# Low parts, one-hot matrices by token pairs, 16-bit index selection and 12 tiles per top-k round in a mixer and expert kernel

## The reference

```
q = (h @ w_query) as [token, 8 heads, 2, 128]
s = q . subkeys                        # 128 scores for each head and half
sv, si = top_k(s, 16)                  # per half
cand   = sv[0][:, None] + sv[1][None]  # 256 sums per head
top_s, pos = top_k(cand, 16)
experts = si[0][pos // 16] * 128 + si[1][pos % 16]
gates   = softmax(top_s)
hid = gelu(u_table[experts] . h) * gates
y   = sum over the 128 chosen of hid * v_table[experts]
```

## Time and profile before

| | |
|---|---|
| median of 3 runs | 3415.35 us (3414.62 to 3419.66) |
| the profiled execution | 3417.07 us, its span 3415.3 us |
| busy share of the span | TensorE 92%, VectorE 70%, GpSimd 38%, ScalarE 34% |
| granted TensorE clock, mean | 0.961 |
| DMA | 542.36 MB, mean 159 GB/s |

### The profile page before, as it was taken

One profiled execution on the slowest core, in us unless ns is written; L12 is line 12 of the kernel. 1 busy time (PEld: TensorE's weight loads), 2 busy tenths in 40 slices (PEclk: granted clock), 3 DMA queues, 4 the chain that ended last, 5 costly groups with the idle time before them and its releaser, 6 DMA issues.

```text
span 3415.3 us, 44166 instructions
## 1 busy us (share of the span) xinstructions
PE 3138.1 (92%) x16765; PEld 2770.9 (81%) x16765; DVE 2400.1 (70%) x3304; ACT 1171.7 (34%) x1668; POOL 1294.8 (38%) x607
## 2 busy tenths in 40 slices
PE   8999997687778777999999999999999999999999
PEld 8788896677777766999999888888888777788887
DVE  6676299999999948799999757454444534445573
ACT  4452343233333332333333332233332435423322
POOL 2303365466676657788888200010000431132000
PEclk9999998898888888999999999999999999999999
DMA  5111354367777688999998133233332321123332
GB/s 171 59 44 56 96 185 134 106 185 248 246 243 232 221 269 303 348 343 343 344 334 314 56 95 96 92 99 95 96 98 91 97 86 38 44 69 95 95 93 93
DMA packets 188077, 542.36 MB, mean 159 GB/s; under 512 B 17696, under 2 KB 77472, under 8 KB 187296
## 3 DMA queue, kind: packets, MB, share of 16 engines
q1 hardware_dynamic: 150112, 403.59, 36.4%
q0 software_dynamic: 36864, 134.23, 11.3%
q10 hardware_dynamic: 960, 2.65, 0.3%
...
...
## 4 chain that ended last, share of the span: by engine, by line
PE 57%; DVE 29%; issue 6%; DMA 5%; ACT 2%; POOL 1%; SPq 0%; DVEq 0%; ACTq 0%
PE ring_banks L295 16%; PE ring_banks L297 16%; PE ring_banks L296 16%; DVE oneI L2874 4%; DVE ge L2896 3%; DVE u_row L2847 3%; DVE row_sum L2857 3%; DMA u_row<-u_rows,row_numbers 2%; DVE glo L2902 2%; DVE vlo L2909 2%; DMA slot<-u 2%; DVE oneJ L2870 1%; DVE hits L2871 1%; PE ring_banks L1635 1%; PE work_banks L1604 1%
## 5 line engine op out<-in xcount | busy, mean ns | idle before, releaser
L915 POOL TENSOR_TENSOR wlo<-slot,whi 128x1024 fp32r<-128x1024 f32 x247 | 650.0, 2636 | 1578.4 <-ACT whi L1747 1577.2
L295 PE MATMUL ring_banks<-xx,wlo 128*128 128x512 f32 (+2 forms) x2704 | 1016.7, 376 | 21.3 <-POOL wlo L915 19.4
L297 PE MATMUL ring_banks<-xx,whi 128*128 128x512 f32 (+2 forms) x2704 | 1002.8, 371 | 0.0
L296 PE MATMUL ring_banks<-xx,whi 128*128 128x512 f32 (+2 forms) x2256 | 832.5, 369 | 0.0
L1747 ACT ACTIVATE whi<-slot 128x1024 fp32r<-128x1024 f32 x427 | 451.5, 1059 | 979.9 <-DMA slot<-w 574.9
L295 PEld LDWEIGHTS ring_banks<-xx,wlo 128*128 128x128 f32 x2704 | 521.8, 193 | 86.5 <-POOL wlo L915 19.8
L297 PEld LDWEIGHTS ring_banks<-xx,whi 128*128 128x128 f32 x2704 | 519.1, 192 | 63.3
L296 PEld LDWEIGHTS ring_banks<-xx,whi 128*128 128x128 f32 x2256 | 436.1, 193 | 46.9 <-issue 0.2
L2322 DVE TENSOR_TENSOR wlo<-slot,whi 128x1024 fp32r<-128x1024 f32 x180 | 220.3, 1224 | 137.2 <-ACT whi L1747 127.3
L2847 DVE SCALAR_TENSOR_TENSOR u_row<-u_row,token_rows 128x1024 f32<-128x1024 f32 x128 | 215.0, 1706 | 75.2 <-DMA u_row<-u_rows,row_numbers 75.1
L2117 ACT ACTIVATE vhi<-v 128x1024 fp32r<-128x1024 f32 x128 | 135.2, 1061 | 335.7 <-DMA v<-v 335.5
...
## 6 DMA issues: line engine op xcount, KB each, us to landing
slot<-w SPq DMA_DIRECT2D x301, 512.0 KB, 3.6
slot<-u SPq DMA_DIRECT2D x128, 512.0 KB, 4.1
v<-v SPq DMA_DIRECT2D x128, 512.0 KB, 7.0
early<-early SPq DMA_DIRECT2D x128, 192.0 KB, 3.9
...
gates<-stage SPq DMA_DIRECT2D x47, 512.0 KB, 5.2
...
```

The source lines that it names most:

```text
L295: pe.matmul(out, w[1], x[0], start=start, stop=False)
L296: pe.matmul(out, w[0], x[1], start=False, stop=False)
L297: return pe.matmul(out, w[0], x[0], start=False, stop=stop)
L915: pool.tensor_tensor(w_lo, slot[s % RING], w_hi.bitcast(F32), ALU.subtract).then_inc(split, 1)
```

## The change

It has four parts. (1) Low parts: VectorE makes all four `vlo` of a group, and the low parts of all U slabs from number AHEAD * 4 on, in the one-hot steps ahead of the rows, and in the tail; GpSimd then only issues row fetches there, as fast as the rings allow. (2) One-hot matrices: `oneI`, `oneJ` and `hits` lie by token pairs, so that the innermost dimension holds two tokens, with step 1 in every operand; the third gate part is bfloat16 too; TensorE reads a token's matrix with a step of two elements. (3) Index selection: `hot`, `sif`, `abf` and the numbers 0 to 15 are bfloat16, the key numbers lie by pairs, and the sum over 16 is made by halving additions, the last of them into float32. (4) AHEAD = 12 and PER_STAGE = 12, so TAIL becomes 8; of each round's 12 tiles 8 stand ahead of the round's exponential on ScalarE, as before.

```diff
-AHEAD = 10
-PER_STAGE = 13
+AHEAD = 12
+TURNS = (AHEAD - 1) // 4
+PER_STAGE = 12
...
+                         name == "u" and slab >= start + AHEAD * TT)
...
+        oneI = halved("oneI", "ones_area", PARTS, PAIRED, P, 2)
+        oneJ = halved("oneJ", "ones_area", PAIRED, P, 2, at=16 * PARTS * P)
+        iota2 = halved("iota2", "iota_area", P, 2)
+        gate3 = halved("gate3", "iota_area", TD, at=2 * P)
+        hits = halved("hits", "sq", BATCH // 2, P, 2)
...
-            u = 16
-            for x in range(ROW_STEPS):
-                until = AHEAD * TT + 2 * (x + 1) * PER_STAGE // 16 + 3
-                while u < until:
-                    split_slab(U_AT + u)
-                    u += 1
-                for s in U_ROWS_AT_STEP[x]:
-                    fetch_u(s + U_RING)
...
+            split_slabs(U_AT + 16, AHEAD * TT - 16)
+            for s in range(U_RING, SLOTS):
+                fetch_u(s)
             pool.wait_ge(done, TILE_AT["hid"] + KEYS)
...
+            for s in range(SLOTS):
+                fetch_v(s)
...
-                            mm = pe.matmul(psB[:, q, u * P:(u + 1) * P], oneI[:, part, 4 * q + u, :],
-                                           oneJ[:, 4 * q + u, :], start=part == 0, stop=part == PARTS - 1)
+                            mm = pe.matmul(psB[:, q, u * P:(u + 1) * P], oneI[:, part, 2 * q + u // 2, :, u % 2],
+                                           oneJ[:, 2 * q + u // 2, :, u % 2], start=part == 0, stop=part == PARTS - 1)
...
+                    step(dve.tensor_tensor(hot, abf[:, x].unsqueeze(2).to_broadcast([P, PEER_HEADS, TOPK, TOPK]),
+                                           ranks.unsqueeze(1).to_broadcast([P, PEER_HEADS, TOPK, TOPK]), ALU.is_equal))
                     step.wait()
...
+                    paired = hot.rearrange("p h a (k e) -> p h a k e", e=2)
+                    step(dve.tensor_tensor(paired, paired, sif[:, x].unsqueeze(3).to_broadcast(
+                        [P, PEER_HEADS, TOPK, TOPK // 2, 2]), ALU.mult))
+                    for half in (8, 4, 2):
+                        step.wait()
+                        step(dve.tensor_tensor(hot[:, :, 0:half, :], hot[:, :, 0:half, :], hot[:, :, half:2 * half, :], ALU.add))
...
-                        return v[:, token:token + BATCH].unsqueeze(2).to_broadcast([P, BATCH, P])
+                        pairs = v[:, token:token + BATCH].rearrange("p (a e) -> p a e", e=2)
+                        return pairs.unsqueeze(2).to_broadcast([P, BATCH // 2, P, 2])
...
+                    for u in range(x * PER_STAGE * BATCH // STAGE, (x + 1) * PER_STAGE * BATCH // STAGE):
+                        slab_low(U_AT + AHEAD * TT + u)
                     for s in U_ROWS_AT_STEP[x]:
                         use_u(s)
...
-            for s in U_ROWS_IN_TAIL:
-                use_u(s)
+            for n in range(TAIL):
+                slab_low(U_AT + KEYS - TAIL + n)
+                for s in U_ROWS_IN_TAIL[n * ROWS_IN_TAIL // TAIL:(n + 1) * ROWS_IN_TAIL // TAIL]:
+                    use_u(s)
...
-                dve.wait_ge(p_vh, 4 * g + 4)
-                dve.tensor_tensor(vlo[b][:, 3, :], vbuf[b][:, 3, :], vhi[b][:, 3, :].bitcast(F32), ALU.subtract).then_inc(p_vd, 1)
+                for r in range(4):
+                    dve.wait_ge(p_vh, 4 * g + r + 1)
+                    dve.tensor_tensor(vlo[b][:, r, :], vbuf[b][:, r, :], vhi[b][:, r, :].bitcast(F32), ALU.subtract).then_inc(p_vs, 1)
```

More of the change, by code:

```diff
@@ L26 @@
 BATCH = 8
+PAIRED = 8
 I32 = mybir.dt.int32
@@ L103, in _low_counts @@
             by_vector = (who and not (name in ("pin0", "cin", "pin1") and slab < start + 7) or
-                         name == "ri" and slab == start + 3)
+                         name == "ri" and slab == start + 3 or
+                         name == "u" and slab >= start + AHEAD * TT)
             n[by_vector] += 1
@@ L490, in build @@
         abu = region("abu", 2, SLOTS)
-        abf = region("abf", 2, SLOTS)
-        hot = region("hot", SLOTS, TOPK)
+        region("abf", SLOTS)
+        abf = halved("abf16", "abf", 2, PEER_HEADS, TOPK)
+        region("hot", PEER_HEADS * 256)
+        hot = halved("hot16", "hot", PEER_HEADS, TOPK, TOPK)
+        sif = halved("sif16", "hot", 2, PEER_HEADS, TOPK, 2, at=PEER_HEADS * 256)
+        ranks = halved("ranks16", "hot", TOPK, TOPK, at=PEER_HEADS * 256 + 4 * SLOTS)
         sel = region("sel", 2, SLOTS)
@@ L922, in split_slabs @@
                     split_slab(s)
-            def split_v(g, r):
-                b = g % 2
-                pool.wait_ge(p_vh, 4 * g + r + 1)
-                pool.tensor_tensor(vlo[b][:, r, :], vbuf[b][:, r, :], vhi[b][:, r, :].bitcast(F32),
-                                   ALU.subtract).then_inc(p_vs, 1)
             def fetch_u(s):
@@ L1442, in _ @@
             for q in range(TT):
-                with pe.Fori(0, AHEAD // 4) as i:
+                with pe.Fori(0, TURNS) as i:
                     for r in range(4):
                         ahead_tile(AHEAD * q + r, i)
-                for r in range(AHEAD // 4 * 4, AHEAD - (q == TT - 1)):
+                for r in range(4 * TURNS, AHEAD - (q == TT - 1)):
                     ahead_tile(AHEAD * q + r)
@@ L2082, in _ @@
                 if q == 0:
-                    for u in range(AHEAD // 4 * 4):
+                    for u in range(4 * TURNS):
                         ahead_gelu(u)
                 else:
-                    with act.Fori(0, AHEAD // 4) as i:
+                    with act.Fori(0, TURNS) as i:
                         for r in range(4):
@@ L2090, in _ @@
                 if q < TT - 1:
-                    for r in range(AHEAD // 4 * 4, AHEAD):
+                    for r in range(4 * TURNS, AHEAD):
                         ahead_gelu(AHEAD * q + r)
@@ L2094, in _ @@
                         take_slots(q - 1)
-            for u in range(AHEAD * (TT - 1) + AHEAD // 4 * 4, AHEAD * TT - 1):
+            for u in range(AHEAD * (TT - 1) + 4 * TURNS, AHEAD * TT - 1):
                 ahead_gelu(u, high=u < AHEAD * TT - 2)
@@ L2772, in gate_parts @@
                 step.wait()
-                step(dve.tensor_tensor(rest2[:, c], rest1[:, c], gate2[:, c], ALU.subtract))
+                step(dve.tensor_tensor(gate3[:, c], rest1[:, c], gate2[:, c], ALU.subtract))
                 step.wait()
@@ L2793, in _ @@
                 step.wait()
-                step(dve.tensor_copy(sif, siu))
+                siu4 = siu.rearrange("p (h x) k -> p h x k", x=2)
+                for x in range(2):
+                    step(dve.tensor_copy(sif[:, x], siu4[:, :, x, :].unsqueeze(3).to_broadcast([P, PEER_HEADS, TOPK, 2])))
                 sv4 = sv.rearrange("p (h x) k -> p h x k", x=2)
@@ L2860, in onehots @@
             def onehots():
-                every = iota16.unsqueeze(1).to_broadcast([P, BATCH, P])
+                every = iota2.unsqueeze(1).to_broadcast([P, BATCH // 2, P, 2])
                 for x in range(ROW_STEPS):
-                    token, b = BATCH * x, BATCH * (x % 2)
+                    token, b = BATCH * x, BATCH // 2 * (x % 2)
                     def row(v):
-                        return v[:, token:token + BATCH].unsqueeze(2).to_broadcast([P, BATCH, P])
+                        pairs = v[:, token:token + BATCH].rearrange("p (a e) -> p a e", e=2)
+                        return pairs.unsqueeze(2).to_broadcast([P, BATCH // 2, P, 2])
                     if token >= 16:
                         dve.wait_ge(p_om, token // 4 - 2)
-                    step(dve.tensor_tensor(oneJ[:, b:b + BATCH, :], every, row(places16[:, 1, :]), ALU.is_equal))
+                    step(dve.tensor_tensor(oneJ[:, b:b + BATCH // 2, :, :], every, row(places16[:, 1, :]), ALU.is_equal))
                     step(dve.tensor_tensor(hits, every, row(places16[:, 0, :]), ALU.is_equal))
                     step.wait()
-                    for part, gate_part in enumerate((gate1, gate2, rest2)):
-                        ins = dve.tensor_tensor(oneI[:, part, b:b + BATCH, :], hits, row(gate_part), ALU.mult)
+                    for part, gate_part in enumerate((gate1, gate2, gate3)):
+                        ins = dve.tensor_tensor(oneI[:, part, b:b + BATCH // 2, :, :], hits, row(gate_part), ALU.mult)
                         if part < PARTS - 1:
```

47 lines of the change are left out of this document (9 added, 38 removed).

## The result

The changed kernel takes **3172.87 us** (median of 4 runs, 3172.35 to 3174.46) against 3416.15 us of the kernel before on the same chip: a ratio of **0.9287**, 95% interval 0.9271 to 0.9303. That is 243 us less; 3188 was predicted, in a range of 3140 to 3290. The profiled execution took 3174.46 us, its span 3172.7.

The account below looks back on a forecast made before the run. VectorE was taken to set the one-hot stage's pace, much of its time lost waiting on GpSimd's low parts, with TensorE also busy in the expert groups. Terms -20 - 148.5 - 25 - 36 = -229.5 from 3417.1 gave 3188 us, range 3140 to 3290.

Parts of the forecast that it names:

- Top-k rounds, -20: Four top-k rounds: cheaper index selection cuts VectorE's round from 57.4 to 50.4 us, level with TensorE's twelve tiles; -20 us.
- two more low parts on GpSimd, a quarter of which meet two-tensor work, add 1.1: Top-k rounds: cost of the extra GpSimd low parts to VectorE, 1.1 us a round, set against 8.4 saved.
- One-hot stage, -148.5: One-hot stage: the step falls from 11.73 to 8.6 us over 47.5 steps, -148.5 us.
- the DMA's 8.36 us: One-hot stage: DMA time for 2.65 MB a step at 317 GB/s; the step was taken a little above it, 8.6.
- VectorE's wait for the high part: One-hot stage: VectorE's new wait for a slab's high part, costed at nothing because a ring of four slabs covers it.
- Tail, -25: Last one-hots to first expert group, 90 us before: fewer tiles -13, VectorE's last rows -12; -25 us (10 to 35).
- six tiles that become four for -13: Tail: after SyncE's next slab, four tiles at 6.7 us each instead of six, -13 us.
- Expert groups, -36: Expert groups: from 18.28 to 17.1 us each over 31, -36 us (0 to -46, the last with TensorE alone).
- (a): Rival: DMA binds throughout, no gain in expert groups, one-hot step of 9.3 us; 3257 us, chance 0.14.
- (b): Rival: pairs bring no second element per cycle, since innermost rows have two elements; VectorE's step 10.4, 3293 us, chance 0.09.
- (c): Rival: GpSimd's row fetches starve beside doubled VectorE operations, two take 10.2 us a step; 3263 us, chance 0.05.
- (d): Rival: TensorE reads the strided one-hots badly; at 0.35 us a matmul the step is 14.8, 3482 us; chance 0.05.

Follow-up runs that it names:

- e1: The change with the one-hot matrices written token by token again, without pairs: 3261.87 us, 0.9538 of the kernel before.
- e2: The change with the later U low parts on GpSimd again, in turn with row fetches: 3292.27 us, 0.9625 of the kernel before.
- e5: The change without GpSimd's low parts of U slabs 16 to 47 in the later rounds, left out of the result: 3152.5 us, 0.9212 of the kernel before.
- e8: The change with three U slabs loaded before and between the gates' way to memory and back in the tail: 3175.78 us, 0.9281 of the kernel before.
- e10: The change with 8 instead of 16 rows of U in the tail, the others in the expert groups: 3160.02 us, 0.9232 of the kernel before.
- e12: The change with no U rows in the tail and three low parts of each of the first three rounds on VectorE: 3145.41 us, 0.9194 of before.

## Why the prediction was right, and where not

*The sum.* That it came within 16 us is in part luck: the rounds and the tail brought 26 us less than forecast, the one-hot stage and the groups 42 more. It also starts from the profiled execution and leaves out the 1.7 us by which that stood above the median, as do the times of the rivals.

*What bounds it.* Right for the kernel before, in both stages. e1 and e2 show the two causes of the one-hot stage apart, and that neither alone is enough there.

*Top-k rounds, -20: wrong, -4.6.* The prices of the new form were right: 1.22, 0.69, 0.42 and 0.29 us free against 1.21, 0.63, 0.35 and 0.2 counted, and without meetings a round takes 47 to 49 us (e5) where 50.4 was worked out. The step that failed is "two more low parts on GpSimd, a quarter of which meet two-tensor work, add 1.1". It counted the two new low parts alone, at an average chance, and priced the selection itself free of meetings, where the 16.8 us a round that it replaces held 3.1 of them. But the selection now is made of two-tensor operations only; the reductions that went, 2.29 us each, had been time in which a low part cost nothing. Of 33 us of free work 60 came, 27 us of meetings in these rows against 12 before (26.6 + 22.4 less 16 x 2.29). Of the 28 us that VectorE was to save in four rounds, 27 less the 4.4 counted went this way; that leaves 5.4, near the 4.6 measured.

*One-hot stage, -148.5: the bound of before was right, the next one was not, and the gain 32 us too small.* VectorE's step was put at 7.5 and takes 7.1 (335.62 of 374 us), TensorE's at 7.7 and takes 7.8 (367.84). The mis-sized term is the DMA's 8.36 us, from which 8.6 was taken: it came from 225 GB/s at a share of 0.71, 317 at a full share, but the stage now carries 325 at 0.95, 342. A step also moves 2.57 MB (325 GB/s in 7.92 us), not 2.65. Why the same engines move more per busy time here no run shows. TensorE, not the DMA engines, sets the step. VectorE's wait for the high part, put at nothing, is 37.3 us in 19 pieces; it fills the 0.8 us a step that VectorE has to spare, and TensorE waits only 4.1 us for `oneI`.

*Tail, -25: -14.* The wait before the first group was put at some 9 and is 8.50 (21.39 before). The other half, six tiles that become four for -13, gave 1. SyncE's queue, timeline:

```profile
1077.93 0.43 SPq L823 DMA_DIRECT2D slot<-u  x1
```

That is 36 us behind the last one-hots, where it was 29, and the four tiles behind it take 8 us each. The step that failed is that four tiles take two thirds of the time of six: the stretch is filled by bytes, 332 GB/s at 0.92, which e8 and e10 show from two sides: another order gains nothing, fewer rows do.

*Expert groups, -36: -45.3.* TensorE alone sets them, 16.6 us in nearly all; 17.1 had left room for the DMA engines. The bound of -46 was named.

*The rivals.* (a) DMA does not bind: 16.6 us a group at a mean of 361 GB/s, and at 407 in e12. (b) Rows of two elements bring the doubled rate: 0.69 us, which is also what was estimated by the Trainium skill (VectorE: DVE Perf Modes, the perf-mode tier table); e1 shows the price without, 1.22, and the cost, 89 us, where (b) had 105 with the rounds. (c) Fetches are not starved: they take 1.31 us in the mean (123.2 us in 94), and GpSimd spends 247 us waiting for rows to be used. The rule of the Trainium skill (SBUF — State Buffer, summary of rules) does not bite with this doubled form: in this stage fetches take 0.93 to 1.69 us. (d) The strided one-hots cost TensorE nothing, 0.87 us for 12 matmuls against 0.84.
